# Other start addresses, by 128 bytes, for the moving operands of three products, and a second view of x

## The reference

```
# hybrid layer, and _mixing in the second block
proj = jnp.einsum("bsd,de->bse", h, w_in)        # 256 x 1024 by 1024 x 3584
...
return x + jnp.einsum("bse,ed->bsd", y, w_out)   # 256 x 1024 by 1024 x 1024
# feed-forward, D_FF = 2816
def _swiglu(h, wg, wu, wd):
    return (jax.nn.silu(h @ wg) * (h @ wu)) @ wd
```

## Time and profile before

| | |
|---|---|
| median of three runs | 1319.07 us (1317.32 to 1320.37) |
| the profiled execution | 1318.59 us |
| its span, first to last instruction | 1316.8 us |
| granted TensorE clock, mean | 0.995 |
| PE busy | 1295.8 us, 98% |
| weight loads busy | 1219.4 us, 93% |
| VectorE, ScalarE busy | 900.4 us (68%), 709.4 us (54%) |
| moved from HBM | 219.2 MB, 167 GB/s |

### The profile page before, as it was taken

The page is one execution under the profiler, slowest core; times in us unless marked ns, Lnnn a source line. Parts: engine busy times, 40 slices in busy tenths (PEclk is TensorE's granted clock), DMA queues, the critical chain, the costliest instruction groups (busy, mean ns, idle before and its releaser), DMA issues.

```text
span 1316.8 us, 23603 instructions
## 1 busy us (share of the span) xinstructions
PE 1295.8 (98%) x9662; PEld 1219.4 (93%) x9662; DVE 900.4 (68%) x1588; ACT 709.4 (54%) x1149; POOL 157.6 (12%) x207
## 2 busy tenths in 40 slices
PE   9999999999999999999999999999999999999997
PEld 7788878999999988899999999999998889999997
DVE  6988798867665577767666566666547876766652
ACT  7664665645454485556444544444458546544441
POOL 3201500382001100012000020000110001200000
PEclk9999999999999999999999999999999999999999
DMA  8635644555556552335555555555645133655560
GB/s 313 202 103 177 215 144 129 176 186 175 182 178 195 175 176 79 122 120 193 179 191 192 177 192 184 186 192 181 200 148 185 59 133 126 197 176 183 188 195 34
DMA packets 61499, 221.77 MB, mean 168 GB/s; under 512 B 7120, under 2 KB 7376, under 8 KB 61136
## 3 DMA queue, kind: packets, MB, share of 16 engines
q1 hardware_dynamic: 60768, 219.00, 50.3%
q0 software_dynamic: 336, 1.11, 0.3%
q10 hardware_dynamic: 288, 0.16, 0.1%
HBM read 219.20 MB, written 1.05 MB: 167 GB/s over the span
## 4 chain that ended last, share of the span: by engine, by line
PE 81%; DVE 10%; issue 3%; POOL 3%; ACT 1%; DMA 1%; SPq 0%; DVEq 0%; ACTq 0%; POOLq 0%
PE pb L473 13%; PE pb L475 13%; PE pb L474 13%; PE pb L488 7%; PE pb L490 7%; PE pb L489 7%; PE pb L457 5%; PE pb L459 5%; PE pb L458 5%; DVE s_wl L1261 3%; DVE s_acc L1394 2%; PE pb L531 2%; PE pb L581 2%; PE pb L704 1%; PE pb L560 1%
## 5 line engine op out<-in xcount | busy, mean ns | idle before, releaser
L1261 DVE TENSOR_TENSOR s_wl<-s_wraw,s_wh 128x1024 fp32r<-128x1024 f32 (+1 forms) x411 | 503.5, 1245 | 115.1 <-ACT s_wh L882 114.8
L882 ACT ACTIVATE s_wh<-s_wraw 128x1024 fp32r<-128x1024 f32 (+1 forms) x411 | 420.9, 1048 | 201.6 <-PE pb L475 113.2
L473 PE MATMUL pb<-s_xh,s_wh 128*128 128x256 f32 x1408 | 399.8, 284 | 0.0
L475 PE MATMUL pb<-s_xh,s_wl 128*128 128x256 f32 x1408 | 399.1, 283 | 0.0
L474 PE MATMUL pb<-s_xl,s_wh 128*128 128x256 f32 x1408 | 399.0, 283 | 0.0
L473 PEld LDWEIGHTS pb<-s_xh,s_wh 128*128 128x128 f32 x1408 | 271.0, 192 | 0.0
L474 PEld LDWEIGHTS pb<-s_xl,s_wh 128*128 128x128 f32 x1408 | 271.0, 192 | 0.0
L475 PEld LDWEIGHTS pb<-s_xh,s_wl 128*128 128x128 f32 x1408 | 270.9, 192 | 0.0
L488 PE MATMUL pb<-s_hh,s_wh 128*128 128x256 f32 x704 | 194.6, 276 | 0.0
L489 PE MATMUL pb<-s_hl,s_wh 128*128 128x256 f32 x704 | 194.5, 276 | 0.0
L490 PE MATMUL pb<-s_hh,s_wl 128*128 128x256 f32 x704 | 194.5, 276 | 0.0
(11 more groups left out here) (302 smaller groups left out, 1515.6 us busy)
## 6 DMA issues: line engine op xcount, KB each, us to landing
s_wraw<-in_w SPq DMA_DIRECT2D x407, 512.0 KB, 4.0
s_nab<-in_rpb SPq DMA_DIRECT2D x2, 1024.0 KB, 8.0
s_x<-in_x SPq DMA_DIRECT2D x4, 256.0 KB, 5.9
out_dram<-s_at_s SPq DMA_DIRECT2D x4, 256.0 KB, 2.3
s_cst<-in_cst SPq DMA_DIRECT2D x1, 684.0 KB, 10.3
s_mlev<-in_lev POOLq DMA_DIRECT2D x1, 576.0 KB, 5.3
s_wraw<-in_w SPq DMA_DIRECT2D x2, 256.0 KB, 4.6
s_ln<-in_lng POOLq DMA_DIRECT2D x2, 128.0 KB, 6.3
```

What stands on the lines that cost most here:

```text
L473: pe.matmul(o, wh[:, s, w], xh[:, k, :], start=k == v == 0, stop=False, skip_group_check=True)
L475: r = pe.matmul(o, wl[:, s, w], xh[:, k, :], start=False, stop=k == 7, skip_group_check=True)
L882: return act.activation(o, src, ACT.Copy, scale=scale)
L1261: dve.tensor_tensor(wl[:, s, part], wraw[:, r, part], wh[:, s, part].bitcast(F32), ALU.subtract).then_inc(low_done, 1)
```

## The change

Four constants say by how many float32 elements a tile begins later: 8 (32 bytes) for the feed-forwards' `hh` and for "mix", 24 (96 bytes) for "b1". They are put in as small unused tiles at the head of the three sets. `s_xh` and `s_xl` become rooms of 8 x 256 + 8 elements with two views each, `x_high(n)` and `x_low(n)`: at 8 elements from the start when phase n is a feed-forward, at 0 otherwise. Behind each room lies a further unused tile of 24 elements, so that what follows keeps its remainder. All writers and readers of x's two parts use the view of their phase. The starts of `s_hh` and `s_hl`, of `y2` and `y2r` have then the remainder 96, those of `y1` 32, and x's two parts 32 in the feed-forwards and 0 in "b1" and "mix". The other tiles of the three sets move by the same 32 or 96 bytes. Nothing else is changed: same instructions, same order, same waits.

```diff
--- before.py
+++ after.py
@@ -122,6 +122,7 @@
 END = len(PHASES)
 RBC_SLOT = {2: 0, 4: 1, 5: 0, 7: 1}
 TURN_STEPS = 62
+XGAP, HGAP, Y1GAP, Y2GAP = 8, 8, 24, 8
 FEEDS = [n for n, (kind, _) in enumerate(PHASES) if kind in ("f1", "f2")]
 NORM = {n: n for n in range(END)}
 NORM[END] = 11
@@ -200,8 +201,18 @@
     wh = sb("wh", [P, NS, UNIT], F32R)
     wl = sb("wl", [P, NS, UNIT], F32R)
     x = sb("x", [P, 8, TOKENS])
-    xh = sb("xh", [P, 8, TOKENS], F32R)
-    xl = sb("xl", [P, 8, TOKENS], F32R)
+    xh_room = sb("xh_room", [P, 8 * TOKENS + XGAP], F32R)
+    sb("gap0", [P, 32 - XGAP])
+    xl_room = sb("xl_room", [P, 8 * TOKENS + XGAP], F32R)
+    sb("gap1", [P, 32 - XGAP])
+
+    def x_high(n):
+        at = XGAP if PHASES[n][0] in ("f1", "f2") else 0
+        return xh_room[:, at:at + 8 * TOKENS].rearrange("p (k t) -> p k t", k=8)
+
+    def x_low(n):
+        at = XGAP if PHASES[n][0] in ("f1", "f2") else 0
+        return xl_room[:, at:at + 8 * TOKENS].rearrange("p (k t) -> p k t", k=8)
     cst = sb("cst", [P, NCST])
     par = sb("par", [P, NPAR])
     mlev = sb("mlev", [P, NLEV], F32R)
@@ -226,6 +237,7 @@
     rbc = sb("rbc", [P, 2, TOKENS])
 
     arena = ExitStack()
+    sb("hgap", [P, HGAP], F32, arena)
     hh = sb("hh", [P, NFT, TOKENS], F32R, arena)
     hl = sb("hl", [P, NFT, TOKENS], F32R, arena)
     gu = sb("gu", [P, 2, 2, TOKENS], F32, arena)
@@ -240,6 +252,7 @@
             self.stat = sb(name + "_stat", [P, 2, 4, 4], F32, where)
 
     arena = ExitStack()
+    sb("y1gap", [P, Y1GAP], F32, arena)
     y1 = [sb(f"y1{j}", [P, 8, TOKENS], F32R, arena) for j in range(2)]
     ha = sb("ha", [P, 2, 256], F32, arena)
     hp = sb("hp", [P, 2, 286], F32, arena)
@@ -272,6 +285,7 @@
     arena.close()
 
     arena = ExitStack()
+    sb("y2gap", [P, Y2GAP], F32, arena)
     y2 = [sb(f"y2{j}", [P, 4, TOKENS], F32R, arena) for j in range(2)]
     exs = [sb("ex0", [P, 2, 8, P], F32, arena)]
     with ExitStack() as inner:
@@ -454,9 +468,9 @@
             for t in range(2):
                 ts = slice(P * t, P * (t + 1))
                 o = (claim(n, ("in", c, t)) if k == 0 else psum(n, ("in", c, t)))[:, :]
-                pe.matmul(o, xh[:, k, ts], hi, start=k == 0, stop=False)
-                pe.matmul(o, xh[:, k, ts], lo, start=False, stop=False)
-                pe.matmul(o, xl[:, k, ts], hi, start=False, stop=k == 7).then_inc(main_done, 1)
+                pe.matmul(o, x_high(n)[:, k, ts], hi, start=k == 0, stop=False)
+                pe.matmul(o, x_high(n)[:, k, ts], lo, start=False, stop=False)
+                pe.matmul(o, x_low(n)[:, k, ts], hi, start=False, stop=k == 7).then_inc(main_done, 1)
 
         def project_features(n, tile, c, k):
             u, j = divmod(tile, TPU)
@@ -470,9 +484,9 @@
                 for v in range(2):
                     w = slice(NCOL * j + P * (2 * i + v), NCOL * j + P * (2 * i + v + 1))
                     o = o2[:, TOKENS * v:TOKENS * (v + 1)]
-                    pe.matmul(o, wh[:, s, w], xh[:, k, :], start=k == v == 0, stop=False, skip_group_check=True)
-                    pe.matmul(o, wh[:, s, w], xl[:, k, :], start=False, stop=False, skip_group_check=True)
-                    r = pe.matmul(o, wl[:, s, w], xh[:, k, :], start=False, stop=k == 7, skip_group_check=True)
+                    pe.matmul(o, wh[:, s, w], x_high(n)[:, k, :], start=k == v == 0, stop=False, skip_group_check=True)
+                    pe.matmul(o, wh[:, s, w], x_low(n)[:, k, :], start=False, stop=False, skip_group_check=True)
+                    r = pe.matmul(o, wl[:, s, w], x_high(n)[:, k, :], start=False, stop=k == 7, skip_group_check=True)
                 r.then_inc(main_done, 1)
 
         def project_out(n, tile, q, pair, first, last):
@@ -730,8 +744,8 @@
             o = claim(n, "ff")
             for k in range(8):
                 w = ffw[:, 64 * l + 8 * k:64 * l + 8 * k + P]
-                pe.matmul(o[:, 0:TOKENS], w, xh[:, k, :], start=k == 0, stop=False)
-                r = pe.matmul(o[:, 0:TOKENS], w, xl[:, k, :], start=False, stop=k == 7)
+                pe.matmul(o[:, 0:TOKENS], w, x_high(n)[:, k, :], start=k == 0, stop=False)
+                r = pe.matmul(o[:, 0:TOKENS], w, x_low(n)[:, k, :], start=False, stop=k == 7)
             r.then_inc(*fill(n, "ff"))
             tiles(n, 3)
             norm_sums(n, 1)
@@ -905,7 +919,7 @@
             if n == FUSED:
                 act.wait_ge(gfg_done, 1)
             for k in (2 * q, 2 * q + 1):
-                copy(xh[:, k, :], x[:, k, :], gain_of(n, k)).then_inc(xh_done, 1)
+                copy(x_high(n)[:, k, :], x[:, k, :], gain_of(n, k)).then_inc(xh_done, 1)
 
         def squares(n, q):
             for kind in range(kinds_of(n)):
@@ -1265,7 +1279,7 @@
         def input_low(n, q):
             for k in (2 * q, 2 * q + 1):
                 dve.wait_ge(xh_done, x_parts(n) + k + 1)
-                dve.scalar_tensor_tensor(xl[:, k, :], x[:, k, :], gain_of(n, k), xh[:, k, :].bitcast(F32), ALU.mult,
+                dve.scalar_tensor_tensor(x_low(n)[:, k, :], x[:, k, :], gain_of(n, k), x_high(n)[:, k, :].bitcast(F32), ALU.mult,
                                          ALU.subtract).then_inc(xl_done, 1)
 
         def next_input(n, scale, at_units):
```

## The result

The changed kernel takes 1324.2 us in the median (1323.5 to 1327.7), the kernel before 1319.1 (1317.1 to 1320.4). The two medians differ by 5.1 us; the ratio over the fast runs is 1.0049, with a 95% interval from 1.0035 to 1.0063. So the changed kernel is slower by some 0.4 to 0.5%, where 2% faster was forecast. Its profiled execution has a span of 1323.1 us, 6.3 more than before.

The account below looks back on a forecast made before the run. TensorE bounds the kernel, through the distance between matmul starts and their number. Gate and up save 27.9 us, all other terms 0: 1318.6 becomes 1290.7, predicted as 1291, range 1260 to 1323.

Parts of the forecast that it names:

- (g): VectorE, ScalarE and DMA keep up with gate and up stretches 5.5% shorter; cover holds, 0.
- What is left is the start address: With shapes, neighbours' load and high/low spacing ruled out, start addresses explain gate and up's 120.0 ns against down's 113.4.
- (a): Gate and up, remainder 0 to 32: 4224 matmuls go from 120.0 to 113.4 ns, saving 27.9 us.
- (f): Gaps, 256 bytes ahead of cst and shifted VectorE and ScalarE tiles: no added instructions, waits or DMA, 0.
- (b): Down, remainder 64 to 96: 2112 matmuls, no change, bounds -10 to +14 us.
- (c): Mixers' output, y1 to remainder 32, y2 and y2r to 96: 768 matmuls, 0, bounds -5 to +4 us.
- (d): Mixers' projection and the forget gate's small product keep their remainders: 0, projection unchanged at 226 ns.
- (e): Transposes, scores, weighing and exponents' product get shifted tiles: 0, the exponents' product 0.5 us either way.
- R2: Closeness to equal remainder counts, from forget gate rows: gate/up -1.3 to -2.2 ns, down/output slower; 1320 to 1326, chance 0.09.
- R5: Remainder is a bystander, placement is worth nothing: 1319, chance 0.07.
- R1: Remainders 32 and 96 avoid the meeting altogether; gate and up at 109 to 111 ns: 1258 to 1272, chance 0.18.

Follow-up runs that it names:

- the version at 112: Kernel before with only x moved: rooms 8448 bytes apart, feed-forwards' view 112 bytes in; 1293.9 us, ratio 0.9803.
- the map: Kernel before plus idle-neighbour matmul streams behind its last matmul, each at its own operand distance, later repeated finer; first pass: distance 96 took 120.0 or 120.1 ns.
- the rooms set right: Changed kernel with x's rooms 8448 bytes apart, a multiple of 256; 1317.2 us, ratio to before 0.9981.
- the finer map: Streams behind the kernel's last matmul at distances 4 bytes apart upward, 8 downward, then 512 columns; distance 192 took 113.3 ns both times.
- the version at 16: Kernel before with x's rooms 8448 bytes apart and feed-forwards' view 16 bytes in; 1317.8 us, ratio 0.9977.

## Why the prediction was wrong

The reading of what bounds the kernel held: TensorE's distance from start to start, with nothing else on the path. In the version at 112 the projected 27.9 us came whole (gate and up 483.0 us instead of 510.9; the median of the total fell by 25.4), so (g) held too: VectorE is busy 63 of 90 us there and gate and up run at 113.3 all through. "What is left is the start address" held as well; down alone, moved by 32 bytes, shows it.

**(a) failed**, and with it the forecast. It took 113.4 for remainder 32 because 64 had it, on the thought that equal remainders by 128 are the one bad case. But that 113.4 was the price of distance 192; distance 64, the same by 128, takes 117.8. Nor does the map show an order in which all but the equal remainder is good: 96 costs as much as 0, 4 costs more, and the good ones (192, 112, at times 16 and 144) lie between bad ones. Of 27.9 us 7.9 came. Part of this was a second mistake, the unit: I took the change's own "by 128 bytes", and (f) passed the 256 bytes ahead of cst as harmless, without noticing that the low part of x moves by 128 bytes of those 256, half a period. With the rooms set right x's part of the change was worth 15.5 us (510.9 to 495.4), still not 27.9, since distance 32 has the rhythm 116.7 and not 113.4.

**(b) failed**: not 0 but +10.0 us, 113.3 to 118.3 ns, inside its bounds (-10 to +14). Its reason, that 96 is as far from equal as 32, again supposed an order by nearness. The rows could not give a value here; they could say that down stood on the lowest rhythm seen, so that an unknown shift had more to lose than to gain. That asymmetry should have moved the forecast.

**(c)** +1.9 us instead of 0, inside its bounds, for the same reason; the second phase went from 113.3 to 116.7. **(d) failed** in a small way: x's low part left distance 0 in the projection, 231 ns instead of 226.7 in steady stretches. The steps under 245 ns have a mean 3 ns longer, some 3.4 us; shorter waits gave half of it back, which leaves 1.7 us in the sum. **(e)** and the rest of (f) held: all other matmuls together took 0.6 us more.

Of the rivals R2 gave the nearest time, 1320 to 1326 with a chance of 0.09, and its two signs are what happened: gate and up -1.5 ns where it had -1.3 to -2.2, down +5.0 where it had +4.4 to +5.3. That was luck, for its mechanism was wrong: nearness does not count (96 takes 120.0 like 0, and 32 takes less than 96). The row it leaned on was read incompletely too: the eight pieces of s_ffw begin 32 bytes apart, so two of eight start at remainder 0, not all at 32, 64 or 96. R5 is refuted by the run with down alone: 2112 matmuls with the same neighbours are 10 us slower for a shift of 32 bytes. The Trainium skill's rule behind it ("SBUF — State Buffer", section "Who interferes with whom") has two parts. That TensorE never waits on anyone is said of the other engines, and no run here contradicts it: the maps show the same rhythms with those engines idle. That its two read ports, one for the moving operand and one for the weight load, are independent does not mean that placement is free: here the distance between the two operands moves a 256-column matmul from 113.3 to 123.4 ns. The result lies 1.2 us above the range's upper end, which cut R2 in the middle. R1's floor of 109 was never reached: no 256-column stream of any map ran under 113.3 with 128 stationary columns.

## What to carry to other kernels

Where TensorE is the bound and moving operands of 256 fp32r columns stream beside 128-column weight loads, look at the distance between the two start addresses by 256 bytes; in this kernel it was worth 2%, and 32 bytes in front of one tile cost 0.8%. If high and low parts of one operand are to have the distance that was chosen, give them rooms that are a multiple of 256 bytes apart. Don't reason from one good or bad distance to its neighbours, and don't trust a distance seen once: map it twice from different histories, for each width on its own.

## What the runs showed of the hardware

At distance 0 moving operands of 256, 384 and 512 columns take 120.0, 173.3 and 226.7 ns at a granted clock of 1.00. That is 53.3 ns for every 128 columns, so streaming alone is 106.7 ns for 256. The excess over it lies between 6.7 and 16.7 ns in the 96 streams of 256 columns in the finer map, most often at 13.3, and repeats with the distance every 256 bytes. A rhythm, once entered, lasts for hundreds of matmuls: down at distance 192 ran whole phases at 113.3 and others at 117.8 in one execution, and gate and up at distance 16 at 116.7 and 118.7. What chooses the rhythm is not shown. Changes of rhythm would account for the spread of the version at 16, 1310.7 to 1321.8 us over its executions, but only one of them has a trace. Where the two operands collide the runs don't tell, nor whether a matmul meets its own weight load or that of the next. They show that the stationary operand's address is part of it, and that it needs neither the other engines nor transfers: behind the first stream of each map these were idle (DMA share 0.22 there, 0.03 and less behind it), and distances 32/160, 112 and 224 had the same values there as in the kernel at work.
